# A two-layer conv and attention trunk with expert retrieval: 32 of the 256 tokens leave the dense expert products and fetch their expert rows by index

## The reference

```python
q = (xt @ w_q).reshape(T, PEER_HEADS, 2, PEER_D_QUERY // 2)
s = jnp.einsum('thpd,pnd->thpn', q, sub_keys)
sv, si = lax.top_k(s, PEER_TOPK)                 # 16 of 128 keys, twice
cand = sv[:, :, 0, :, None] + sv[:, :, 1, None, :]
cv, ci = lax.top_k(cand.reshape(T, PEER_HEADS, 256), PEER_TOPK)
...
experts = (i1 * PEER_N_KEYS + i2)                # (T, 8 heads * 16) of 16384 experts
gates = jax.nn.softmax(cv, axis=-1)
ub = jnp.take(u, eb, axis=0)                     # 128 rows of u for each token
a = jax.nn.gelu(jnp.einsum('td,tkd->tk', xb, ub)) * gb
vb = jnp.take(v, eb, axis=0)
y = jnp.einsum('tk,tkd->td', a, vb)
```

## Time and profile before

| | |
|---|---|
| median of 3 runs | 1806.92 us (1805.59 to 1807.14) |
| span of the profiled execution | 1805.5 us |
| PE, PEld busy | 1791.5 us (99%), 1570.1 us (87%) |
| DVE busy | 1366.3 us (76%) |
| ACT busy | 945.6 us (52%) |
| POOL busy | 212.6 us (12%) |
| DMA | 323.89 MB, mean 179 GB/s |
| chain that ended last | PE 89%, DVE 7%, DMA 1%, rest 3% |

### The profile page before, as it was taken

How to read it: one execution, slowest core, us unless ns; L and a number is a source line. 1 busy time by engine, 2 the same in 40 slices (tenths; PEclk the granted TensorE clock), 3 DMA queues, 4 the chain that set the end, 5 groups by cost and what they waited for, 6 DMA issues and landing times.

```text
span 1805.5 us, 28004 instructions
## 1 busy us (share of the span) xinstructions
PE 1791.5 (99%) x10622; PEld 1570.1 (87%) x10622; DVE 1366.3 (76%) x2461; ACT 945.6 (52%) x1489; POOL 212.6 (12%) x122
## 2 busy tenths in 40 slices
PE   9999999999999999999999999999999999999998
PEld 9889998888888888888888899988888888888886
DVE  7975999888986665666666669998889866666665
ACT  5565445555555455555535454555555554555552
POOL 6720930000000000000004048000000000000000
PEclk9999999999999999999999999999999999999999
DMA  7544555555556566667733346555555566666772
GB/s 240 184 152 153 186 174 168 165 172 166 169 171 211 192 195 195 199 219 245 241 111 116 111 152 195 170 161 171 165 175 164 175 212 196 193 192 207 220 217 79
DMA packets 89413, 323.89 MB, mean 179 GB/s; under 512 B 10048, under 2 KB 10560, under 8 KB 89024
## 3 DMA queue, kind: packets, MB, share of 16 engines
q1 hardware_dynamic: 85248, 307.42, 53.3%
q10 hardware_dynamic: 4032, 14.68, 2.3%
HBM read 321.01 MB, written 1.05 MB: 178 GB/s over the span
## 4 chain that ended last, share of the span: by engine, by line
PE 89%; DVE 7%; DMA 1%; issue 1%; ACT 1%; POOL 0%; SPq 0%; DVEq 0%; ACTq 0%
PE y L662 40%; PE work L553 19%; PE work L556 10%; PE work L594 9%; PE y L934 3%; DVE y L1691 3%; PE work L612 2%; PE y L640 2%; PE work L615 1%; PE work L802 1%; PE y L907 1%; DMA raw<-conv_in 1%; DMA raw<-v 0%; DVE far_homes L483 0%; DMA raw<-u 0%
## 5 line engine op out<-in xcount | busy, mean ns | idle before, releaser
L483 DVE TENSOR_TENSOR low<-raw,high 128x1024 fp32r<-128x1024 f32 x385 | 470.6, 1224 | 136.8 <-ACT high L978 132.2
L978 ACT ACTIVATE high<-raw 128x1024 fp32r<-128x1024 f32 x431 | 453.5, 1053 | 198.3 <-PE work L556 97.6
L553 PE MATMUL work<-xT,high 128*128 128x512 f32 x1472 | 374.0, 396 | 0.1
L662 PE MATMUL y<-high,xT 128*128 128x512 f32 x1296 | 352.6, 390 | 0.0
L553 PEld LDWEIGHTS work<-xT,high 128*128 128x128 f32 x1472 | 264.1, 189 | 47.6 <-DVE low L483 0.5
L662 PE MATMUL y<-far_homes,xT 128*128 128x512 f32 x1320 | 304.8, 390 | 0.2 <-DVE xT L1603 0.2
L662 PEld LDWEIGHTS y<-far_homes,xT 128*128 128x128 f32 x1320 | 247.1, 188 | 51.7 <-DVE far_homes L483 0.6
L662 PEld LDWEIGHTS y<-high,xT 128*128 128x128 f32 x1296 | 243.0, 188 | 50.2
L1244 ACT ACTIVATE xT<-big 128x256 fp32r<-128x256 f32 x256 | 105.3, 416 | 256.8 <-PE y L662 251.4
L556 PEld LDWEIGHTS work<-xT,low 128*128 128x128 f32 x1472 | 200.8, 190 | 14.6
L556 PE MATMUL work<-xT,low 128*128 128x256 f32 x1472 | 205.0, 282 | 0.0
(11 more groups left out here) (208 smaller groups left out, 1818.8 us busy)
## 6 DMA issues: line engine op xcount, KB each, us to landing
raw<-u SPq DMA_DIRECT2D x256, 512.0 KB, 3.6
raw<-v SPq DMA_DIRECT2D x256, 512.0 KB, 4.3
raw<-wq SPq DMA_DIRECT2D x32, 512.0 KB, 3.7
raw<-conv_in SPq DMA_DIRECT2D x14, 512.0 KB, 4.4
aux<-ln_par ACTq DMA_DIRECT2D x9, 512.0 KB, 6.5
raw<-conv_out SPq DMA_DIRECT2D x8, 512.0 KB, 4.0
raw<-mla_out SPq DMA_DIRECT2D x8, 512.0 KB, 4.7
big<-diag ACTq DMA_DIRECT2D x6, 512.0 KB, 6.2
```

The source lines that it names most:

```text
L483: ops.tensor_tensor(low_at(c), raw[:, slot, :], high_at(c).bitcast(F32), ALU.subtract).then_inc(low_made[slot], 1)
L553: nc.tensor.matmul(both, w_high[:, cols], xT[:, k], start=(k == 0), stop=False)
L662: mm = nc.tensor.matmul(y[:, 2 * h + m, :], a[:, a_slot, rows], v[:, m * 512:(m + 1) * 512], start=(start and n == 0), stop=(stop and n == 2))
L978: A(high_at(c), raw[:, slot, :], ACT.Copy).then_inc(high_made, 1)
```

## The change

In both layers the last 32 tokens (`SIDE`) take no part in the dense products of the u stage, which then has `DT` = 224 tokens. Their 128 experts each are fetched: POOL copies their choice and their x into a layout of 4 groups of 32 partitions, and issues 64 indirect DMAs in a layer, 32 of u rows and 32 of v rows, each of 128 rows of 4 KB (512 KB), into three buffers. DVE multiplies and sums each (32 dot products in blocks 2 to 56 of the v stage, 32 weighted sums in blocks 60 to 114), and PE adds the sum over the four groups by two matmuls with a selector. In the v stage the columns of these tokens in the stationary tile are zero; the matmuls there keep their number and their width.

The u stage has 39 early blocks and 44 pairs instead of 35 and 46, and 28 batches instead of 32: one behind each of pairs 0 to 7, then 4 in 7 pairs. Of the two lows that are made beside a pair (n, n + 1), that of block n + 4 stays on DVE and that of block n + 5 goes to POOL, up to the last two pairs. POOL makes 28 lows in the early part instead of 24. The growth of the lead in the v stage starts at block 71. The attention's weights are issued at blocks 107, 111 and 115 of the v stage, not at 94, 100 and 106.

```diff
-EARLY = 35
+EARLY = 39
 PAIRS = (NKEYS - 1 - EARLY) // 2
-CHOSEN_AT = 33
+CHOSEN_AT = 37
-PICK_LOWS = (27, 33)
+PICK_LOWS = (31, 37)
+SIDE = 32
+DT = T - SIDE
+SIDE_ROWS = PH * TOPK // SIDE_GROUPS
+SIDE_BUFS = 3
+SIDE_DOTS_AT = {2 + _d * 7 // 4: _d for _d in range(SIDE_ROWS)}
+SIDE_GELU_AT = 58
+SIDE_SUMS_AT = {60 + _d * 7 // 4: _d for _d in range(SIDE_ROWS)}
-PAIR_OF = [_b if _b < DENSE else DENSE + (_b - DENSE) * 3 // 2 for _b in range(BATCHES)]
+PAIR_OF = [_b if _b < DENSE else DENSE + (_b - DENSE) * 7 // 4 for _b in range(BATCHES)]
-GROW_FROM, GROW_EVERY = 63, 8
+GROW_FROM, GROW_EVERY = 71, 8
...
@@ gpsimd
                 low_stage(u0 + RING, u0 + PICK_LOWS[0])
+                pool.wait_ge(own_picked, layer + 1)
+                for g in range(SIDE_GROUPS):
+                    at = slice(SIDE * g, SIDE * (g + 1))
+                    nc.gpsimd.dma_start(picks[at], own_picks[SIDE_AT:P, :, SIDE_ROWS * g:SIDE_ROWS * (g + 1)]
+                                        ).then_inc(picks_in, 16)
+                    nc.gpsimd.dma_start(side_x[at], x[SIDE_AT:P, 1, :]).then_inc(side_x_in, 16)
+                for pair in range(PAIRS - 2):
+                    make_low(pool, nc.gpsimd, u0 + EARLY + 2 * pair + 5)
...
+                def gather(n):
+                    before = 2 * SIDE_ROWS * layer + n
+                    if before >= SIDE_BUFS:
+                        pool.wait_ge(side_used, before - SIDE_BUFS + 1)
+                    rows, at = (u_rows, n) if n < SIDE_ROWS else (v_rows, n - SIDE_ROWS)
+                    nc.gpsimd.indirect_dma_start(
+                        out=side_rows[before % SIDE_BUFS], out_offset=None, in_=rows,
...
@@ tensor, project_merged (project_block alike)
-                        nc.tensor.matmul(both, w_high[:, cols], xT[:, k], start=(k == 0), stop=False)
+                        nc.tensor.matmul(both, w_high[:, cols], xT[:, k, :, 0:DT], start=(k == 0), stop=False)
...
-                        mm = nc.tensor.matmul(both[:, 0, :], w_low[:, cols], xT_high[:, k, :],
+                        mm = nc.tensor.matmul(both[:, 0, :], w_low[:, cols], xT_high[:, k, 0:DT],
@@ tensor, combine_second_half
+                if norm % 2 == 1:
+                    pe.wait_ge(selector_ok, norm // 2 + 1)
+                    pe.wait_ge(side_used, 2 * SIDE_ROWS * (norm // 2 + 1))
+                    for m in range(2):
+                        nc.tensor.matmul(y[:, 2 + m, :], selector, side_sum[:, m * 512:(m + 1) * 512],
+                                         start=False, stop=False)
@@ vector, gate_blocks
                     if more:
                         make_onehots(layer, b + 2)
-                    if pair + 1 < PAIRS:
+                    if pair == PAIRS - 2:
                         make_low(dve, V, u0 + n + 5)
@@ vector, combine
+                def side_dot(d):
+                    rows = rows_of(before + d)
...
+                    V.scalar_tensor_tensor(rows, rows, 1.0, side_x, ALU.mult, ALU.mult,
+                                           accum_out=side_hid[:, d:d + 1]).then_inc(side_used, 1)
...
                 for c in range(v0, end - TAIL):
+                    if c - v0 in SIDE_DOTS_AT:
+                        side_dot(SIDE_DOTS_AT[c - v0])
+                    if c - v0 in SIDE_SUMS_AT:
+                        side_weighted(SIDE_SUMS_AT[c - v0])
```

More of the change, by code:

```diff
@@ L195, in program @@
 def program(nc, x_rows, x_cols, positions, conv_par, diag, mla_par, ln_par, keys, w_uq, w_uk, w_uv,
-            blocks, out):
+            u_rows, blocks, out):
     with ExitStack() as ctx:
@@ L231, in room @@
             return flat if dtype is None else flat.bitcast(dtype)
+        hid = room(0, NKEYS * DT).rearrange("p (b t) -> p b t", t=DT)
+        side_x = room(112, D)
+        side_sum = side_x
+        side_rows = [room(116 + 4 * n, D) for n in range(SIDE_BUFS)]
+        own_picks = room(127, 2 * P).rearrange("p (s k) -> p s k", s=2)
+        pick_ids = picks[:, 0, :].bitcast(I32)
+        selector = cross[:, 0, 0:P]
         iota = room(126, P)
@@ L479, in make_low @@
         def make_low(eng, ops, c):
-            slot = c % RING
+            slot = c % RAW
             eng.wait_ge(high_made, c + 1)
@@ L564, in project_block @@
                 if name[0] == "u":
-                    out_ = work[:, bank_of(c - first), 0:T]
+                    out_ = work[:, bank_of(c - first), 0:DT]
                     if c == first + NKEYS - 1:
@@ L1613, in combine, with rows_of, side_weighted @@
                 done = v0 + RING
+                before = 2 * SIDE_ROWS * layer
+                step(V.memset(selector, 0.0))
+                for g in range(SIDE_GROUPS):
+                    at = slice(SIDE * g, SIDE * (g + 1))
+                    last = V.tensor_copy(selector[at, SIDE_AT:P], ident[at, at])
+                last.then_inc(selector_ok, 1)
+                def rows_of(n):
+                    dve.wait_ge(side_in[n % SIDE_BUFS], 16 * (n // SIDE_BUFS + 1))
+                    return side_rows[n % SIDE_BUFS]
+                def side_dot(d):
+                    rows = rows_of(before + d)
+                    if d == 0:
+                        dve.wait_ge(side_x_in, 16 * SIDE_GROUPS * (layer + 1))
+                    V.scalar_tensor_tensor(rows, rows, 1.0, side_x, ALU.mult, ALU.mult,
+                                           accum_out=side_hid[:, d:d + 1]).then_inc(side_used, 1)
+                def side_weighted(d):
+                    n = before + SIDE_ROWS + d
+                    weight = side_hid[:, d:d + 1]
+                    if d == 0:
+                        dve.wait_ge(side_gelu, layer + 1)
+                        step(V.tensor_tensor(side_hid[:], side_hid[:], picks[:, 1, :], ALU.mult))
+                    rows = rows_of(n)
+                    dve.wait_ge(side_used, n)
+                    if d == 0:
+                        V.tensor_scalar(side_sum, rows, weight, None, ALU.mult).then_inc(side_used, 1)
+                    else:
+                        V.scalar_tensor_tensor(side_sum, rows, weight, side_sum, ALU.mult,
+                                               ALU.add).then_inc(side_used, 1)
                 for c in range(v0, end - TAIL):
+                    if c - v0 in SIDE_DOTS_AT:
+                        side_dot(SIDE_DOTS_AT[c - v0])
+                    if c - v0 in SIDE_SUMS_AT:
+                        side_weighted(SIDE_SUMS_AT[c - v0])
                     if layer == 0 and c - v0 + RING in ANGLES_AT:
```

115 lines of the change are left out of this document (73 added, 42 removed).

## The result

The changed kernel takes 1823.89 us (median of 4 runs, 1820.2 to 1831.32) against 1806.93 for the kernel before beside it (1805.59 to 1807.14): a ratio of 1.0098, interval 1.0084 to 1.0111. It is slower by 17 us where I forecast 21 us less.

The account below looks back on a forecast made before the run. PE was taken to bound the kernel, busy 99%, with DVE one step behind. Terms -45.4 + 16 + 2 + 4 + 2 = -21.4 us against 1805.5 gave 1784.1, median 1785.5, said as 1786; range 1757 to 1858.

Parts of the forecast that it names:

- The columns: u stage: 448-column matmuls take 202 ns instead of 230, 224-column ones stay at 119; 19.5 us a layer less in pairs.
- rival 4: u stage: narrow matmuls gain too, 105 ns each, 23 us a layer more; time 1762 to 1775, chance 0.13.
- The lock: u-stage pairs: lows on POOL shut out DVE operations reading SBUF on both sides; 8 us a layer later, bounds 0 and 43.
- The v stage's DMA: v stage: gathers beside loads bring the DMA share to 0.89, 0.94 during growth; 2 us a layer allowed, 4 in all.
- rival 3: v stage: gathers make it wait for loads, each costing 1.2 of a load; 27 us a layer, 1836, chance 0.13.
- DVE in the v stage: v stage: 64 DVE operations of 1.3 us fit, 2.40 of 2.72 us a block; 2 us allowed for layer 0's angles.
- The range: Whole kernel: 1757 us (224-column matmuls gain, DVE never late) to 1858 (POOL's lows lock DVE in full).

Follow-up runs that it names:

- experiment 10: Kernel before with its dense u products on 128 of the 256 token columns, the other half not computed: 1741.06 us, one run.
- experiment 8: Kernel before with u-stage matmuls of 224 and 448 columns instead of 256 and 512; batches, lows and v unchanged: 1754.16 us, ratio 0.9712.
- experiment 3: Changed kernel with the 42 lows of a layer moved from POOL back to DVE: 1797.08 us, ratio 0.9934 to the kernel before.
- experiment 5: Changed kernel with both the 42 lows of a layer back on DVE and free room 64 for block 131: 1782.84 us, ratio 0.9869.
- experiment 1: Changed kernel without its indirect DMAs, row buffers zeroed once a layer, DVE's dot products and sums kept: 1785.92 us, ratio 0.9886.
- experiment 2: Changed kernel with all gathers, but DVE's dot products and weighted sums on 32 of 1024 columns: 1801.47 us, ratio 0.9962.
- experiment 4: Changed kernel with one more far home, free room 64, for block 131 (attention's first weights): 1812.15 us, ratio 1.0032.
- experiment 9: Changed kernel with no fetches (buffers zeroed), all lows back on DVE and a room for block 131: 1750.11 us, ratio 0.9684.

## Why the prediction was wrong, step by step

- **The columns** (forecast 19.5 us a layer in the pairs, nothing from the narrow matmuls). The wide term was right, 205 ns for 202. The narrow one came out between my 119 ns and rival 4's 105: 110 ns, a gain of 9 ns each, and experiment 10 shows a floor there. It paid in the pairs; the early blocks of experiment 8 shortened by 2.5 us where 35 x 24 x 8 ns would be 6.7, since the selection on DVE sets their end (106.0 us with 224 columns, 105.7 with 128).
- **The lock** (forecast 8 us a layer). The mechanism and the mean price of one low were right, 1.5 us of DVE for my 1.45. But in the eight pairs where it matters most the low did not lie beside the additions from PSUM, it came behind the one-hot row and cost 2.1 (3.38 - 1.28), and a pair took 6.76 us there (300.31 to 307.07). So the term was mis-sized, 11 to 13 us a layer (experiments 3 and 5), some 2 of them by the clock: by the pieces of the chain the changed pairs and the last early block are 250 us of matmuls and take 266. Experiment 8 shows the other half of what I missed: my 6.36 us of DVE for a pair with a batch were 5.8 to 6.1, so DVE was hardly a bound without POOL's help, and the hand-over had nothing to give. The upper bound of this term was also added up wrong: by its own figures it is 8 x 1.4 + 5 x 7.7 = 50 us a layer and not 43. All the same the u stages came out 3 to 4 us a layer better than forecast, since the narrow columns paid for it.
- **The v stage's DMA** (forecast 4 us in all). This is the step that failed: the v stages lost 53 us, and 38 us of the run hang on the fetches (experiment 1). The shares that I added were about right: 0.85 measured for 0.89 to 0.94. The conclusion from them was not. I allowed for a wait only where the share comes near 1, but a load is late long before: it had 1.5 us to spare, and now takes 5.2 us in the median and 5.4 to 8.1 in the chain instead of 4.3. I had written that argument down under rival 3, and set the 282 GB/s at 0.81 against it; that window had nearly the same share without dot products in DVE's queue, and lasted 20 us. Rival 3 gives the loss in size (54 forecast for 53), but that is luck: it comes from a share over 1, and there was none. A fetch occupies the engines for 28.4% of 200 us over 39 fetches, 1.5 us, against 1.6 for a load, so 0.9 of one and not 1.2, and the loss of the first v stage has the room of block 131 in it.
- **DVE in the v stage** (forecast nothing, 2 us for the angles). Right by itself: 1217 and 1279 ns each and 1.8 us in the second layer without fetches. Wrong beside late loads, where the same operations cost another 5 to 14 us (experiment 2). I costed the two one at a time, and both lie in the same round.
- **The room of block 131** (not in the forecast). No part of the forecast has it, since I took the table of rooms for bookkeeping. The first v stage tells 6 to 7 us: 7.2 in experiment 4, 361.6 - 355.2 = 6.4 between experiments 1 and 9 (which also differ in the lows). The medians tell more, 11.7 in experiment 4 and 14.2 between 3 and 5, with the scatter of the late loads in them. So its size is not settled better than 6 to 14.
- **The range.** Its lower end of 1757 us, given as rival 4 with no lateness on DVE, doesn't come out of the terms: 1785.5 - 16 - 2 x 23 is 1723.

The account of the stages closes: -24.3 and -25.4 in the pairs, +6.5 twice in the early blocks, +30.2 and +23.1 in v make +16.6, against 17.0 in the medians. The shares of the causes within v are less sure, since executions of one kernel differ by 3 to 20 us once the loads are late (1820.2 to 1831.3 us for the changed kernel, 1787.2 to 1806.6 in experiment 3, 1805.6 to 1807.1 before).

## What to carry to other kernels

A mean share of 0.85 on the DMA engines does not tell whether a ring of three slots keeps up: count the round instead (load, rounding, remainder, what stands ahead of them in the queue, the next issue) and compare it with three blocks of the bound engine (here 8.2 us). Cost additions to one such round together, since two that each fit into its slack may not fit both. And before work is handed from VectorE to GpSimd to relieve it, work out whether the shared time costs more than the work itself: here 1.5 us for a remainder of 1.22. When durations of a timeline are added up, compare the sum with the distance between two starts: here 6.36 against 5.84.

## What the runs showed of the hardware

- An fp32r matmul with 128 columns of weights has a floor of 110 ns: 128 and 224 columns cost the same, 256 cost 118 to 120, 448 cost 205.
- GpSimd and VectorE hold each other up both ways. An f32 subtraction on GpSimd that started 0.08 us behind a VectorE f16 operation took 3.40 us, one that started ahead of it 2.39; the VectorE f16 operations behind them took 3.38 instead of 1.28 and 2.98 instead of 1.22. The section "Who interferes with whom" of the Trainium skill's "SBUF — State Buffer" lets the first to start hold the pair for its whole instruction. These rows agree: the 3.40 are the 1.13 us that VectorE's operation still had to run and 2.27 of GpSimd's own.
- A fetch of 128 rows of 4 KB by index cost this kernel more than one of 128 neighbouring rows, at a lower share of the DMA engines: 23 us over 128 fetches, 0.18 us each, by loads of the other queue that land later (5.2 us in the median for 4.7). The cause is open.
